# A two-layer decoder trunk on one core: nine chunks of the odd input projection moved between the steps of the differential attention

## The chip, the cores and the metric

The kernel runs on one NeuronCore of one Trainium2 chip, in float32 throughout. The metric is the device time of one execution in microseconds. Large matrix products are made in three matmuls each, from a high and a low part of both operands (high times high, low times high, high times low), so that the single-pass float format reaches nearly float32 accuracy.

## The reference, cut to what matters

Two transformer layers on 512 tokens of width 1024. Each layer has a half-step feed-forward block, a mixer, a cross-attention to a memory of 256 tokens, and another half-step feed-forward block, each between a norm before and a norm after it. The change lies in the mixer of the second (odd) layer:

```python
def odd_mixer(h, w_in, w_out, q_norm, kv_norm, w_uq, w_ukv, lam, subln, rel_tab, lam_init):
    c_q, c_kv, k_rope, qd, kd, vd = split_cols(h @ w_in, OD_SIZES)
    o_c = mla_mixer(c_q, c_kv, k_rope, q_norm, kv_norm, w_uq, w_ukv)
    o_d = diff_mixer(qd, kd, vd, lam, subln, rel_tab[:, A_HEADS + B_HEADS:], lam_init)
    return jnp.concatenate([o_c, o_d], axis=-1) @ w_out

# diff_mixer, per block of 128 queries; q and k have two parts e per head, v one of width 128
s = jnp.einsum('bthed,bshed->behts', qb, k) * scale + rel_bias(dist, tab)
p = masked_softmax(s, dist >= 0)
a = p[:, 0] - lam_full * p[:, 1]
o = jnp.einsum('bhts,bshd->bthd', a, v)
o = rmsnorm(o, subln) * (1.0 - lam_init)
```

`h @ w_in` has 2048 padded output columns, 16 chunks of 128: two for c_q, one for c_kv, one for k_rope, four each for the queries, keys and values of the four differential heads.

## The kernel before, in words

Everything is kept transposed: a chunk is 128 features on the partitions by 512 tokens. The kernel is written by hand for each engine, with semaphores between them; nothing but that written order decides when something runs.

**The weight stream.** A chunk's weights (128 x 1024, 512 KB) are a unit. SP loads units into a ring of four raw buffers (`stream`, L530); GpSimd splits each into `w_hi` (L604) and `w_lo` (L606) in a ring of four (`split`, `units`), as soon as TensorE has finished the unit four before; TensorE makes 8 products of three matmuls from it (`product`, L755 to L757) and signals `unit_done`; VectorE then takes the bank out, times the norm factor r (`leave`, L1742), and signals `chunk_out`.

**The odd mixer** (`odd_mixer` in each engine's block). TensorE makes chunks 0 to 3 in halves inside `pre_norm`, chunk 4 in a spare bank (7), and then all others in turn through banks 0 to 3 (`chunks`). Between them stand the column sums (L783) and transposes (L791) for the norms of c_q and c_kv. VectorE takes the chunks out, makes the norms' inverse roots (`rsqrt`, L1613 to L1631), scales c_q and c_kv (L1975) and forms their low parts `cq_lo` and `ckv_lo` (L1980). When all 16 chunks are made, TensorE transposes the four value chunks (`turn_rows`, L964) in banks 6 and 7, and ScalarE copies them to `diff_v` (`copy_rows`, L1362).

**The differential attention** (`attention(2)`). 32 jobs in this order: head, block of 128 queries i (with 128(i+1) keys), part e. Each is a pipeline over steps; in step s
- TensorE makes the logits of job s (L993), the transposes of job s-4 (L1007) and the value product of job s-6 (L1024); the last two only for e = 1, where both parts have been joined;
- VectorE inverts the row sum of job s-3 (L1844) and scales its probabilities (L1860 for e = 0, L1854 for e = 1, joined with those of e = 0), and adds the bias to the logits of job s and finds their maximum (L1834);
- ScalarE copies the transposed probabilities of job s-4 (L1413) and makes the exponentials of job s (L1400).

Logits go through banks 0, 1, 2 and 5 in turn (`B_S`), outputs through 3 and 4 by head, r through 5. Behind the last step ScalarE takes the last head out (L1422, L1423), TensorE makes the column sums of the subnorm (L1182) and goes on with the query up-projection of MLA (L755 to L757 from `cq_hi`, `cq_lo`), whose results VectorE and GpSimd turn into rotary queries; then comes the MLA attention, with the same pipeline.

Of the kernel before, what the change touches and what calls it, by code (L numbers as in the profile page):

```python
# [27 lines left out]
P = 128  # L28
D, T, MEM, DFF, DEPTH = 1024, 512, 256, 2816, 2
KC = D // P  # L30
NT = T // P
# [3 lines left out]
A_HEADS, B_HEADS, C_HEADS, D_HEADS, X_HEADS = 8, 8, 8, 4, 4  # L35
# [15 lines left out]
R = 4  # L51
# [12 lines left out]
IQ, IK, VG, KB, QB, KCMP, VCMP, KS, VS, KW, VW, QA = 0, 2, 3, 4, 5, 9, 10, 11, 12, 13, 14, 15  # L64

CQ, CKV, KR, DQ, DK, DVT = 0, 2, 3, 4, 8, 12


C_ID, C_CAUSAL, C_ROPE, C_END = 0, P, P + T, P + 3 * T
# [49 lines left out]
def build(nc, a):  # L119
# [151 lines left out]
    def bank_of(name, c, half=0):  # L271

        kind = name.rstrip("0123")
        if kind in ("up", "ev_in", "od_in") and c == R:
            return B_SPARE
        if kind == "down" and c == KC - 1 and half == 1:
            c -= 1
        return (CHUNK[name] + c) % R
# [8 lines left out]
    def post_buf(s, c):  # L287

        return (step[0], step[1], sq[0], sq[1])[c - 4] if len(HALVED[s]) > 1 else sq[1]
    B_S = [(0, 1, 2) if n == 3 else (0, 1, 2, 5) for n in range(5)]  # L290

    sems = {}

# [185 lines left out]
    def out_rows(phase, f):  # L479

        if JOBS[phase][0][0] != "mla":
            return slice(0, P), f
        return slice(DV // 2 * (f % 2), DV // 2 * (f % 2) + DV // 2), f // 2

    def probs_of(phase, s):

# [33 lines left out]
    with nc.Block() as block:  # L520
# [230 lines left out]
        def _(pe):  # L751
# [205 lines left out]
                    half_sums(8, 1)  # L957
                    turn_half(8, 1)

            def turn_rows(key, k, src, tiles):  # L960

                n = TURN[key] + k
                for i in range(tiles):
                    mm = pe.transpose(bank[B_T[n % 2]][:, P * i:P * i + P], src[:, P * i:P * i + P], ident[:])  # L964
                mm.then_inc(turned, 1)

            def attention(phase, hooks={}):
# [4 lines left out]
                def logit(s):  # L972
                    j, info = j0 + s, infos[s]
                    banks = B_S[phase]
                    if s >= len(banks):
                        pe.wait_ge(logit_done, j - len(banks) + 1)
                    if info["mask"] is not None and JOBS[phase][s][1] == 0:
                        pe.wait_ge(mask_done, JOBS[phase][s][2])
                    if phase == 2 and s == 3:
                        pe.wait_ge(lo_done, SPLIT["ckv"] + 1)  # L980
                    out = bank[banks[s % len(banks)]][:, 0:info["w"]]
                    if phase == 0 and JOBS[0][s][2] == 0 and JOBS[0][s][0] in ("slc", "dsa"):
                        pe.wait_ge(q_lo_done, info["strip"] + 1)
                    if phase == 0 and s in (1, 2, 3, 4):
                        pe.wait_ge(k_lo_pool, 2 * s)
                    if phase == 0 and JOBS[0][s] == ("dsa", 0, 0):
                        pe.wait_ge(k_lo_pool, 9)
                    more = info["mask"] is not None
                    if info["k_lo"] is not None:
                        pe.matmul(out, info["q"], info["k"], start=True, stop=False)  # L990
                        mm = pe.matmul(out, info["q"], info["k_lo"], start=False, stop=not more)
                    else:
                        mm = pe.matmul(out, info["q"], info["k"], start=True, stop=not more)  # L993
                    if info["mask"] is not None:
                        mm = pe.matmul(out, ident_bf[:], info["mask"], start=False, stop=True)
                    mm.then_inc(qk_done, 1)

                def turn(s):
                    j, info = j0 + s, infos[s]
                    if not info["turns"]:  # L1000
                        return
                    t, prob = info["turn"], probs_of(phase, s)
                    pe.wait_ge(scaled, j + 1)
                    if t >= infos[0]["turn"] + 2:
                        pe.wait_ge(probT_copied, t - 1)
                    for b in range(info["blocks"]):
                        mm = pe.transpose(bank[B_T[t % 2]][0:info["rows"], P * b:P * b + P],  # L1007
                                          prob[:, P * b:P * b + info["rows"]], ident[:])
                    mm.then_inc(probT_done, 1)
# [146 lines left out]
            def odd_mixer(s):  # L1156
                pre_norm(s, "od_in")
                c0 = CHUNK["od_in"]
                chunks("od_in", 8, R + 1, h_hi, h_lo)
                pe.wait_ge(sq_done, SQ["cq", 0]["sq"] + 2)  # L1160
                sums(sq[0], NT, True, False)
                sums(sq[1], NT, False, True).then_inc(stat_done, 1)
                chunks("od_in", 12, 8, h_hi, h_lo)
                turn_r(("cq", 0), NT)
                pe.wait_ge(sq_done, SQ["ckv", 0]["sq"] + 1)
                sums(sq[0], NT, True, True).then_inc(stat_done, 1)
                chunks("od_in", OD_IN, 12, h_hi, h_lo)
                pe.wait_ge(mla_ready, 2)
                turn_r(("ckv", 0), NT)
                for h in range(D_HEADS):  # L1170
                    if h >= 2:
                        pe.wait_ge(rows_done, V_ROWS["dv"] + h - 1)
                    pe.wait_ge(chunk_out, c0 + DVT + h + 1)
                    turn_rows("dv", h, od[:, DVT + h, :], NT)
                pe.wait_ge(rows_done, V_ROWS["dv"] + D_HEADS)
                attention(2)

                pe.wait_ge(sub_sq, D_HEADS)
                for h in range(D_HEADS):
                    for i in range(NT):  # L1180
# [71 lines left out]
        def _(act):  # L1252
# [102 lines left out]
                        act.activation(gate[p][:], gate[p][:], ACT.Silu).then_inc(silu_done, 1)  # L1355
                halved_squares(s + 1, f"down{f}", y_ffn)

            def copy_rows(key, k, dst, tiles):
                n = TURN[key] + k
                act.wait_ge(turned, n + 1)  # L1360
                src = bank[B_T[n % 2]][:, 0:P * tiles].rearrange("p (i t) -> p i t", i=tiles)
                act.activation(dst, src, ACT.Copy).then_inc(rows_done, 1)  # L1362

            def copy_half(key, k, dst, frm, to):
# [13 lines left out]
                for k in range(len(STRIPS[phase][1])):  # L1378
                    load_strip(phase, k)

            def attention(phase, hooks={}):
                infos, j0 = INFO[phase], JOB0[phase]
                logits, _, probTs = BUFS[phase]
                if phase in STRIPS:
# [41 lines left out]
                        act.activation(h_hi[rows, chunk, :], src[rows, :], ACT.Copy).then_inc(hi_done, 1)  # L1426

                for s in range(len(infos) + OUT_AT + 1):
                    if TURN_AT <= s < len(infos) + TURN_AT:
                        copy(s - TURN_AT)  # L1430
                    if s < len(infos):
                        exp(s)
                    if s > OUT_AT and infos[s - OUT_AT - 1]["ends"]:
                        output_leaves(s - OUT_AT - 1)
                    if s in hooks:
                        hooks[s]()
# [81 lines left out]
            def odd_mixer(s):  # L1518
# [3 lines left out]
                for k in range(2):  # L1522
                    act.wait_ge(chunk_out, c0 + CQ + k + 1)
                    act.activation(sq[k][:], od[:, CQ + k, :], ACT.Square).then_inc(sq_done, 1)
                act.wait_ge(stat_done, SQ["cq", 0]["stat"] + 1)
                act.activation(sq[0][:], od[:, CKV, :], ACT.Square).then_inc(sq_done, 1)
                for k in range(2):
                    act.wait_ge(mla_ready, k + 1)
                    act.activation(cq_hi[:, k, :], od[:, CQ + k, :], ACT.Copy).then_inc(hi_done, 1)
                for h in range(D_HEADS):  # L1530
                    copy_rows("dv", h, dv[:, h, :, :], NT)
                act.wait_ge(mla_ready, 3)
                act.activation(ckv_hi[:], od[:, CKV, :], ACT.Copy).then_inc(hi_done, 1)
                attention(2)
                act.wait_ge(logit_done, JOB0[3])
                act.dma_start(rope_t[:], a["consts"][:, C_ROPE:C_END].rearrange("p (k t) -> p k t", k=2)).then_inc(aux_in, 16)
                act.dma_start(od_causal[:], a["consts"][:, C_CAUSAL:C_CAUSAL + T]).then_inc(aux_in, 16)
# [55 lines left out]
        def _(dve):  # L1593
# [367 lines left out]
            def odd_mixer(s):  # L1961
                def leave_to(c0, c1):
                    for c in range(c0, c1):
                        leave("od_in", c, c + 1, od[:, c, :], r_sb[:])


                leave_to(0, 8)
                dve.wait_ge(chunk_out, CHUNK["od_in"] + 8)
                for key, d, cs, g0, lo in ((("cq", 0), 2 * P, (CQ, CQ + 1), G_Q, (cq_lo[:, 0, :], cq_lo[:, 1, :])),
                                           (("ckv", 0), P, (CKV,), G_KV, (ckv_lo[:],))):  # L1970
                    rsqrt(key, NT, d)
                    leave_to(*((8, 12) if key[0] == "cq" else (12, OD_IN)))
                    dve.wait_ge(r_turned, SQ[key]["rt"] + 1)
                    for k, c in enumerate(cs):
                        dve.scalar_tensor_tensor(od[:, c, :], od[:, c, :], gains[:, g0 + k:g0 + k + 1], bank[B_RT][:],  # L1975
                                                 ALU.mult, ALU.mult).then_inc(mla_ready, 1)
                    for k, c in enumerate(cs):
                        hi = cq_hi[:, k, :] if key[0] == "cq" else ckv_hi[:]
                        dve.wait_ge(hi_done, SPLIT[key[0]] + k + 1)
                        dve.tensor_tensor(lo[k], od[:, c, :], hi.bitcast(F32), ALU.subtract).then_inc(lo_done, 1)  # L1980
                attention(2)
                rsqrt(("sub", 0), NT * D_HEADS, DV)

                dve.wait_ge(aux_in, AUX["od"])
# [170 lines left out]
```

## Time and profile before

| | us |
|---|---|
| median of 3 runs | 2337.35 (2337.11 to 2339.36) |
| the profiled execution | 2340.13 |
| its span | 2338.2 |
| TensorE busy | 2239.3 (96%) |
| VectorE busy | 1233.2 (53%) |
| ScalarE busy | 541.8 (23%) |
| GpSimd busy | 1368.7 (59%) |

PE is TensorE, DVE VectorE, ACT ScalarE, POOL GpSimd, SP the engine that issues weight loads; PEld is TensorE's loading of stationary operands. Busy times of TensorE are modelled: its matmuls overlap, so the distance between starts is the better measure of what one takes. A float32 matmul of the attention appears as two records, and so does one of the column sums. PEclk is the granted clock of TensorE as a share of 2.4 GHz; it has two levels, 1.00 and 0.50. All positions are us from the span's start. The odd mixer's projection begins near 1567 us and its differential attention ends near 1712 us.

### The profile page before, as it was taken

The numbers are of one execution on the slowest core, as the hardware profiler recorded it, in microseconds if no ns is written. First come the engines' busy times: TensorE is split into PE (matmuls) and PEld (weight loads), VectorE is DVE, ScalarE is ACT, GpSimd is POOL, SyncE is SP. The second block draws the span as 40 slices with busy tenths as digits, with TensorE's granted clock in tenths as the row PEclk, the third lists the DMA queues.
The fourth block names the chain that finished last, engine by engine and source line by source line (L and its number), as shares of the span: only waits on it lengthen the run. The fifth ranks groups of instructions, "written<-read, shape, count | busy, mean of one in ns | idle before, by whom it ended". The sixth has DMA issues, their size and how long they took to land.

```text
span 2338.2 us, 32876 instructions
## 1 busy us (share of the span) xinstructions
PE 2239.3 (96%) x11598; PEld 1893.0 (81%) x11598; DVE 1233.2 (53%) x2370; ACT 541.8 (23%) x1313; POOL 1368.7 (59%) x850
## 2 busy tenths in 40 slices
PE   6999999999999899999999999999989989999997
PEld 5888888778878788888898888888667879888886
DVE  5554324798865575543247454243577645645323
ACT  2101003228742441110030000021346144101000
POOL 5666665671347376666667666666231745766662
PEclk9999999999999999999999999999889999999998
DMA  5433332310123123333323333333111311333331
GB/s 192 170 94 95 92 98 81 131 46 20 46 85 105 55 73 99 99 96 93 98 67 112 95 98 92 99 88 104 50 50 36 109 55 54 109 98 92 93 98 52
DMA packets 62146, 205.61 MB, mean 88 GB/s; under 512 B 6815, under 2 KB 9247, under 8 KB 61652
## 3 DMA queue, kind: packets, MB, share of 16 engines
q1 hardware_dynamic: 55312, 187.86, 26.9%
q10 hardware_dynamic: 6724, 16.29, 2.0%
q8 instruction: 68, 1.11, 0.2%
q14 instruction: 42, 0.34, 0.0%
HBM read 201.98 MB, written 8.70 MB: 90 GB/s over the span
## 4 chain that ended last, share of the span: by engine, by line
PE 85%; DVE 10%; issue 2%; ACT 2%; POOL 1%; DMA 0%; SPq 0%; DVEq 0%; ACTq 0%; POOLq 0%
PE bank L755 25%; PE bank L757 25%; PE bank L756 25%; PE bank L1024 3%; PE bank L1007 2%; PE bank L993 1%; POOL sq_sum L630 1%; DVE ev_logit L1834 1%; DVE h_lo L1647 1%; DVE top L1931 1%; PE bank L783 1%; DVE bank L1708 1%; PE bank L807 1%; DVE od_logit L1834 0%; DVE x_res L1716 0%
## 5 line engine op out<-in xcount | busy, mean ns | idle before, releaser
L606 POOL TENSOR_TENSOR w_lo<-w_raw,w_hi 128x1024 fp32r<-128x1024 f32 (+1 forms) x358 | 866.5, 2420 | 29.9
L755 PE MATMUL bank<-h_hi,w_hi 128*128 128x512 f32 (+1 forms) x2136 | 804.5, 377 | 27.8 <-DVE h_lo L1647 11.5
L756 PE MATMUL bank<-h_lo,w_hi 128*128 128x512 f32 (+1 forms) x2136 | 797.4, 373 | 0.0
L757 PE MATMUL bank<-h_hi,w_lo 128*128 128x512 f32 (+1 forms) x2136 | 797.3, 373 | 0.0
L604 POOL TENSOR_SCALAR w_hi<-w_raw 128x1024 fp32r<-128x1024 f32 (+1 forms) x358 | 383.6, 1071 | 687.2 <-PE bank L757 522.3
L755 PEld LDWEIGHTS bank<-h_hi,w_hi 128*128 128x128 f32 x2136 | 408.4, 191 | 106.5 <-issue 16.4
L757 PEld LDWEIGHTS bank<-h_hi,w_lo 128*128 128x128 f32 x2136 | 408.2, 191 | 69.5
L756 PEld LDWEIGHTS bank<-h_lo,w_hi 128*128 128x128 f32 x2136 | 409.1, 192 | 67.8
L755 PE MATMUL bank<-act_hi,w_hi 128*128 128x512 f32 (+1 forms) x792 | 290.1, 366 | 0.0
L756 PE MATMUL bank<-act_lo,w_hi 128*128 128x512 f32 (+1 forms) x792 | 289.4, 365 | 0.0
L757 PE MATMUL bank<-act_hi,w_lo 128*128 128x512 f32 (+1 forms) x792 | 289.4, 365 | 0.0
L1783 DVE TENSOR_TENSOR up<-bank,r_tok 128x512 f32<-128x512 f32 x88 | 60.6, 689 | 346.7 <-PE bank L757 346.7
L1355 ACT ACTIVATE gate<-gate 128x512 f32<-128x512 f32 x88 | 55.6, 632 | 758.3 <-DVE gate L1781 758.2
L1788 DVE TENSOR_SCALAR act_hi<-up 128x512 f32 (+1 forms) x88 | 192.8, 2191 | 11.8 <-DVE up L1786 11.2
L1759 DVE COPY y_ffn<-bank 128x512 f32<-128x512 f32 x28 | 19.4, 691 | 310.6 <-PE bank L757 310.6
L756 PEld LDWEIGHTS bank<-act_lo,w_hi 128*128 128x128 f32 x792 | 149.4, 189 | 24.3
L755 PEld LDWEIGHTS bank<-act_hi,w_hi 128*128 128x128 f32 x792 | 149.3, 189 | 24.2
L757 PEld LDWEIGHTS bank<-act_hi,w_lo 128*128 128x128 f32 x792 | 149.3, 189 | 23.8
L1750 DVE TENSOR_TENSOR sq_sum<-sq_sum,sq 128x512 f32<-128x512 f32 x42 | 103.0, 2452 | 27.9 <-ACT sq L1333 27.9
L1786 DVE TENSOR_TENSOR up<-gate,up 128x512 f32<-128x512 f32 x88 | 103.4, 1175 | 6.5 <-ACT gate L1355 1.3
L1333 ACT ACTIVATE sq<-y_ffn 128x512 f32<-128x512 f32 x24 | 15.2, 633 | 343.8 <-DVE y_ffn L1759 343.8
L1790 DVE TENSOR_TENSOR act_lo<-up,act_hi 128x512 f32 (+1 forms) x88 | 76.1, 865 | 9.4
(275 smaller groups left out, 2421.6 us busy)
## 6 DMA issues: line engine op xcount, KB each, us to landing
w_raw<-in_w_up SPq DMA_DIRECT2D x176, 512.0 KB, 3.6
w_raw<-in_w_down SPq DMA_DIRECT2D x64, 448.0 KB, 3.3
w_raw<-in_w_down SPq DMA_DIRECT2D x32, 512.0 KB, 3.5
w_raw<-in_w_ev_in SPq DMA_DIRECT2D x19, 512.0 KB, 3.6
w_raw<-in_w_xkv SPq DMA_DIRECT2D x16, 512.0 KB, 3.5
w_raw<-in_w_od_in SPq DMA_DIRECT2D x16, 512.0 KB, 3.5
bias_line_rows<-bias_lines ACTq DMA_DIRECT2D x1, 6400.0 KB
ev_strip<-bias_line_rows ACTq DMA_DIRECT2D x16, 256.0 KB, 2.9
```

The source lines that it names most:

```text
L604: pool.tensor_scalar(w_hi[j][:, 0:cols], raw[j][:, 0:cols], 1.0, 0.0, ALU.mult, ALU.add).then_inc(hi_split, 1)
L606: pool.tensor_tensor(w_lo[j][:, 0:cols], raw[j][:, 0:cols], w_hi[j][:, 0:cols].bitcast(F32), ALU.subtract).then_inc(split_done, 1)
L755: pe.matmul(out, w_hi[j][:, w], hi, start=first, stop=False)
L756: pe.matmul(out, w_hi[j][:, w], lo, start=False, stop=False)
L757: return pe.matmul(out, w_lo[j][:, w], hi, start=False, stop=last)
L1024: mm = pe.matmul(bank[B_O[chunk % 2]][features, tokens], v, probTs[t % N_PROBT][0:info["rows"], P * b:P * b + P], start=info["opens"] and ...
L1355: act.activation(gate[p][:], gate[p][:], ACT.Silu).then_inc(silu_done, 1)
L1750: dve.tensor_tensor(sq_sum[:], sq_sum[:], sq[c % 2][:], ALU.add).then_inc(sq_added, 1)
L1783: dve.tensor_tensor(up[p][:], bank[(c0 + k + 1) % R][:], r_sb[:], ALU.mult).then_inc(chunk_out, 1)
L1786: dve.tensor_tensor(up[p][:], gate[p][:], up[p][:], ALU.mult).then_inc(prod_done, 1)
L1788: dve.tensor_scalar(act_hi[:, 2 * i + n, :], up[p][:], 1.0, None, ALU.mult).then_inc(act_hi_done, 1)
L1790: dve.tensor_tensor(act_lo[:, 2 * i + n, :], up[p][:], act_hi[:, 2 * i + n, :].bitcast(F32), ALU.subtract).then_inc(act_done, 1)
```

## The change

Only chunks 0 to 6 are made before the attention; the other nine (7 to 15) are made inside it, one to three products at the end of each of its 32 steps (`OD_FILL`: 3 in each of the first eight, 3 and 2 in turn in the next sixteen, 1 in each of the last eight). The order of the weights' chunks is changed on the host, so that the first seven are c_q, c_kv and then query, key and value of head 0 and the query of head 1; then key and value of head 1 and so on, and k_rope last. The nine chunks alternate between banks 0 and 1, and the logits of this attention have banks 2 and 5 only. VectorE takes each of the nine out at the end of the step after the one in which it ends. The value chunks of heads 1 to 3 are transposed at the end of steps 6, 16 and 24, in the transposes' bank that is not in use, and copied by ScalarE at the start of the same steps in its own order. The sums for the norm of c_q come before chunk 5, those for c_kv before chunk 6.

```diff
+OD_ORDER = (CQ, CQ + 1, CKV) + tuple(t + h for h in range(D_HEADS) for t in (DQ, DK, DVT)) + (KR,)
+OD_FIRST = 7
+OD_FILL = (3,) * 8 + (3, 2) * 8 + (1,) * 8
@@ bank_of
+        if kind == "od_in" and c >= OD_FIRST:
+            return (c + 1) % 2
-    B_S = [(0, 1, 2) if n == 3 else (0, 1, 2, 5) for n in range(5)]
+    B_S = [(0, 1, 2, 5), (0, 1, 2, 5), (2, 5), (0, 1, 2), (0, 1, 2, 5)]
@@
+    fill_of, fill_end, n_fill = [], {}, 8 * OD_FIRST
+    for at_step, count in enumerate(OD_FILL):
+        fill_of.append([divmod(n, KC) for n in range(n_fill, n_fill + count)])
+        n_fill += count
+        for c, k in fill_of[-1]:
+            if k == KC - 1:
+                fill_end[c] = at_step
+    DV_STEP = {h: 2 * (fill_end[OD_ORDER.index(DVT + h)] // 2) + 2 for h in range(1, D_HEADS)}
+    def dv_bank(h):
+        return B_T[(INFO[2][DV_STEP[h] - TURN_AT - 1]["turn"] + 1) % 2 if h else TURN["dv"] % 2]
@@ TensorE, attention
-                    if phase == 2 and s == 3:
-                        pe.wait_ge(lo_done, SPLIT["ckv"] + 1)
+                    if phase == 2 and s == 1:
+                        pe.wait_ge(mla_ready, 3)
+                    if phase == 2 and JOBS[2][s][2] == 0 and JOBS[2][s][0] == "diff0":
+                        pe.wait_ge(chunk_out, CHUNK["od_in"] + OD_ORDER.index(DK + JOBS[2][s][1]) + 1)
...
+                    if phase == 2 and s + TURN_AT - 1 in DV_STEP.values():
+                        pe.wait_ge(rows_done, V_ROWS["dv"] + 1 + list(DV_STEP.values()).index(s + TURN_AT - 1) + 1)
@@ TensorE, odd_mixer
-                chunks("od_in", 8, R + 1, h_hi, h_lo)
                 pe.wait_ge(sq_done, SQ["cq", 0]["sq"] + 2)
                 sums(sq[0], NT, True, False)
                 sums(sq[1], NT, False, True).then_inc(stat_done, 1)
-                chunks("od_in", 12, 8, h_hi, h_lo)
+                u0 = UNIT["od_in"]
+                chunk_of_unit(u0 + 5, c0 + 5, (u0 + 5) % R, bank_of("od_in", 5), h_hi, h_lo)
                 turn_r(("cq", 0), NT)
                 pe.wait_ge(sq_done, SQ["ckv", 0]["sq"] + 1)
                 sums(sq[0], NT, True, True).then_inc(stat_done, 1)
-                chunks("od_in", OD_IN, 12, h_hi, h_lo)
+                pe.wait_ge(chunk_out, c0 + OD_ORDER.index(DVT) + 1)
+                turn_rows("dv", 0, od[:, DVT, :], NT)
+                chunk_of_unit(u0 + 6, c0 + 6, (u0 + 6) % R, bank_of("od_in", 6), h_hi, h_lo)
                 pe.wait_ge(mla_ready, 2)
                 turn_r(("ckv", 0), NT)
-                for h in range(D_HEADS):
-                    if h >= 2:
-                        pe.wait_ge(rows_done, V_ROWS["dv"] + h - 1)
-                    pe.wait_ge(chunk_out, c0 + DVT + h + 1)
-                    turn_rows("dv", h, od[:, DVT + h, :], NT)
-                pe.wait_ge(rows_done, V_ROWS["dv"] + D_HEADS)
-                attention(2)
+                pe.wait_ge(rows_done, V_ROWS["dv"] + 1)
+                def fill(step_):
+                    for h, at_ in DV_STEP.items():
+                        if at_ == step_:
+                            pe.wait_ge(chunk_out, c0 + OD_ORDER.index(DVT + h) + 1)
+                            turn_rows("dv", h, od[:, DVT + h, :], NT, dv_bank(h))
+                    for c, k in fill_of[step_] if step_ < len(fill_of) else ():
+                        if k == 0:
+                            pe.wait_ge(split_done, u0 + c + 1)
+                            pe.wait_ge(chunk_out, c0 + c - 1)
+                        mm = product(bank_of("od_in", c), (u0 + c) % R, k, h_hi[:, k, :], h_lo[:, k, :],
+                                     k == 0, k == KC - 1)
+                        if k == KC - 1:
+                            mm.then_inc(unit_done, 1)
+                attention(2, {n: lambda n=n: fill(n) for n in range(len(JOBS[2]))})
+                pe.wait_ge(chunk_out, c0 + OD_IN)
@@ ScalarE, odd_mixer
-                for h in range(D_HEADS):
-                    copy_rows("dv", h, dv[:, h, :, :], NT)
+                copy_rows("dv", 0, dv[:, 0, :, :], NT)
...
-                attention(2)
+                attention(2, early={at_: lambda h=h: copy_rows("dv", h, dv[:, h, :, :], NT, dv_bank(h))
+                                    for h, at_ in DV_STEP.items()})
@@ VectorE, odd_mixer
-                leave_to(0, 8)
-                dve.wait_ge(chunk_out, CHUNK["od_in"] + 8)
+                leave_to(0, 5)
+                dve.wait_ge(chunk_out, CHUNK["od_in"] + 5)
...
-                    leave_to(*((8, 12) if key[0] == "cq" else (12, OD_IN)))
+                    leave_to(*((5, 6) if key[0] == "cq" else (6, 7)))
...
-                attention(2)
+                attention(2, {at_ + 1: lambda c=c: leave_to(c, c + 1) for c, at_ in fill_end.items()})
+                dve.wait_ge(chunk_out, CHUNK["od_in"] + OD_IN)
@@ host
-    ins["w_od_in"] = tiles(np.concatenate(cols, 1), KC, OD_IN)
+    ins["w_od_in"] = tiles(np.concatenate(cols, 1), KC, OD_IN)[list(OD_ORDER)]
```

## Rows read from the trace of the kernel before

**Rows 1.** The page's chain that ended last, by engine.
```profile
PE 85%; DVE 10%; issue 2%; ACT 2%; POOL 1%; DMA 0%; SPq 0%; DVEq 0%; ACTq 0%; POOLq 0%
```

**Rows 2.** Windows: length; busy PE, PEld, DVE, ACT, POOL; PEclk; DMA share, GB/s.
```profile
1663.50:1712.30 48.80, 39.04 (x201) 26.48 (x198) 35.50 (x147) 32.04 (x93) 0.00 (x0) 0.79 0.04 13
1667.50:1709.20 41.70, 33.04 (x161) 21.62 (x161) 34.01 (x145) 28.19 (x86) 0.00 (x0) 0.78 0.03 7
1713.40:1724.60 11.20, 11.18 (x44) 10.08 (x45) 4.43 (x14) 0.00 (x0) 0.00 (x0) 0.55 0.20 69
431.00:457.00 26.00, 24.97 (x132) 17.00 (x125) 23.73 (x29) 10.71 (x24) 12.60 (x8) 1.00 0.28 82
1750.00:1780.00 30.00, 29.44 (x203) 23.81 (x202) 26.58 (x96) 23.97 (x70) 0.00 (x0) 1.00 0.05 18
```

**Rows 3.** Timeline of TensorE around the attention: start, us, what, [idle before].
```profile
1663.35 1.04 PE L964 MATMUL bank<-ident,od_proj 128*128 128x128 f32 x8
...
1666.47 0.92 PE L993 MATMUL bank<-od_proj 64*128 64x128 f32 x6 [0.69 <-ACT diff_v L1362]
...
1707.26 0.63 PE L1007 MATMUL bank<-ident,od_prob 128*128 128x128 f32 x3 [2.02 <-DVE od_prob L1854]
```

**Rows 4.** Timeline of VectorE in the projection: chunks 5 and 6 leave.
```profile
1605.51 0.69 DVE L1742 TENSOR_TENSOR od_proj<-bank,r_tok 128x512 f32<-128x512 f32 x1 [4.75 <-PE bank L757]
1610.95 0.69 DVE L1742 TENSOR_TENSOR od_proj<-bank,r_tok 128x512 f32<-128x512 f32 x1 [4.75 <-PE bank L757]
```

**Rows 5.** Chain in order of time, attention stages: start, us, what.
```profile
1687.84 1.16 PE bank L993 x4
...
1692.11 0.89 PE bank L1024 x8
1693.00 1.11 PE bank L993 x4
...
1762.45 0.44 PE bank L1007 x4
```

**Rows 6.** The same chain in the projection: sums, r transposes, next matmul.
```profile
1616.35 1.68 PE bank L783 x16
...
1639.95 0.44 PE bank L791 x4
1640.39 0.79 PE bank L783 x8
1641.18 0.34 PE bank L755
```

**Rows 7.** VectorE's cq_lo (ns min/median/max), and GpSimd's timeline beside it.
```profile
L1980 DVE TENSOR_TENSOR cq_lo<-od_proj,cq_hi x2: 678/1439/2200, 1642.0 to 1644.2; 128x512 fp32r<-128x512 f32 x2
...
1640.15 1.05 POOL L604 TENSOR_SCALAR w_hi<-w_raw 128x1024 fp32r<-128x1024 f32 x1 [1.91 <-PE bank L757]
1641.29 2.40 POOL L606 TENSOR_TENSOR w_lo<-w_raw,w_hi 128x1024 fp32r<-128x1024 f32 x1
```

**Rows 8.** Timeline of TensorE in the even mixer: twelve matmuls between small ones.
```profile
431.18 0.50 PE L755 MATMUL bank<-h_hi,w_hi 128*128 128x512 f32 x1
...
434.13 0.71 PE L1085 MATMUL bank<-ev_proj 32*128 32x256 f32 x8
```

**Rows 9.** Chain in order of time, from the second last logit to the sums.
```profile
1704.46 0.67 DVE od_logit L1834
...
1712.28 0.35 ACT diff_o L1422
...
1713.42 6.11 PE bank L1182 x32
```

**Rows 10.** The same chain behind the sums: two matmuls of the query projection.
```profile
1720.60 0.43 PE bank L757
...
1725.06 0.24 PE bank L756
```

**Rows 11.** VectorE's logit group, 1667.5 to 1709.2: busy, mean ns, idle before.
```profile
L1834 DVE CUSTOM_DVE_ANT_0 od_logit<-bank,od_strip 128x128 f32<-128x128 f32 (+3 forms) x32 | 15.4, 486 | 5.4 <-PE bank L993 5.4
```

More of the change, by code:

```diff
@@ L483, in out_rows @@
         return slice(DV // 2 * (f % 2), DV // 2 * (f % 2) + DV // 2), f // 2
+    fill_of, fill_end, n_fill = [], {}, 8 * OD_FIRST
[5 more added lines that the diff above has]
+                fill_end[c] = at_step
+    assert n_fill == KC * OD_IN
+    DV_STEP = {h: 2 * (fill_end[OD_ORDER.index(DVT + h)] // 2) + 2 for h in range(1, D_HEADS)}
+    def dv_bank(h):
+        return B_T[(INFO[2][DV_STEP[h] - TURN_AT - 1]["turn"] + 1) % 2 if h else TURN["dv"] % 2]
     def probs_of(phase, s):
@@ L958, in ffn, with turn_rows @@
                     turn_half(8, 1)
-            def turn_rows(key, k, src, tiles):
+            def turn_rows(key, k, src, tiles, to=None):
                 n = TURN[key] + k
+                to = B_T[n % 2] if to is None else to
                 for i in range(tiles):
-                    mm = pe.transpose(bank[B_T[n % 2]][:, P * i:P * i + P], src[:, P * i:P * i + P], ident[:])
+                    mm = pe.transpose(bank[to][:, P * i:P * i + P], src[:, P * i:P * i + P], ident[:])
                 mm.then_inc(turned, 1)
@@ L1356, in ffn, with copy_rows @@
                 halved_squares(s + 1, f"down{f}", y_ffn)
-            def copy_rows(key, k, dst, tiles):
+            def copy_rows(key, k, dst, tiles, frm=None):
                 n = TURN[key] + k
                 act.wait_ge(turned, n + 1)
-                src = bank[B_T[n % 2]][:, 0:P * tiles].rearrange("p (i t) -> p i t", i=tiles)
+                src = bank[B_T[n % 2] if frm is None else frm][:, 0:P * tiles].rearrange("p (i t) -> p i t", i=tiles)
                 act.activation(dst, src, ACT.Copy).then_inc(rows_done, 1)
@@ L1379, in first_strips, with attention @@
                     load_strip(phase, k)
-            def attention(phase, hooks={}):
+            def attention(phase, hooks={}, early={}):
                 infos, j0 = INFO[phase], JOB0[phase]
@@ L1428, in attention @@
                 for s in range(len(infos) + OUT_AT + 1):
+                    if s in early:
+                        early[s]()
                     if TURN_AT <= s < len(infos) + TURN_AT:
@@ L1524, in odd_mixer @@
                     act.activation(sq[k][:], od[:, CQ + k, :], ACT.Square).then_inc(sq_done, 1)
+                act.wait_ge(chunk_out, c0 + CKV + 1)
                 act.wait_ge(stat_done, SQ["cq", 0]["stat"] + 1)
@@ L1963, in leave_to @@
                     for c in range(c0, c1):
-                        leave("od_in", c, c + 1, od[:, c, :], r_sb[:])
-                leave_to(0, 8)
-                dve.wait_ge(chunk_out, CHUNK["od_in"] + 8)
+                        leave("od_in", c, c + 1, od[:, OD_ORDER[c], :], r_sb[:])
+                leave_to(0, 5)
+                dve.wait_ge(chunk_out, CHUNK["od_in"] + 5)
                 for key, d, cs, g0, lo in ((("cq", 0), 2 * P, (CQ, CQ + 1), G_Q, (cq_lo[:, 0, :], cq_lo[:, 1, :])),
```

## Prediction

> **What bounds the kernel now.** I read the page's chain of waits first: 85% of the span is TensorE, 10% VectorE [rows 1]. So a change is worth what it takes out of TensorE's sequence at the place where it acts. Next the windows by stage. In the differential attention with what leads into it (1663.5 to 1712.3 us) TensorE is busy 39.0 of 48.8 us at a mean granted clock of 0.79, and GpSimd does nothing [rows 2]. The timeline shows why: TensorE waits for VectorE's scaled probabilities (2.02 us before 1707.26) and, at the start, for ScalarE's copies of the values (0.69) [rows 3]. The projection before it has no such holes: its chunks leave at a steady 5.44 us [rows 4]. The change puts projection work into the hole. What can be won is the hole (idle time, and time lost to the half clock), less what the interleaving costs.
>
> **Work per piece.** A chunk is 24 matmuls and takes 5.44 us (its results leave at 1605.51 and 1610.95) [rows 4]; nine are 48.96 us, before and after. A product (three matmuls) is 0.68 us. The attention's own TensorE work at the full clock, by head [rows 5]: logits have four records of each width; 512 columns take 1.11, 256 columns 1.16 at the half clock, so 0.58, 384 between them 0.84, and 128 columns I put at the 0.11 a record of the value product: 3.0 us. Ten transposes at 0.11 (four in 0.44) are 1.1, twenty records of the value product at 0.11 (eight in 0.89) 2.2. That is 6.3 us a head, 25.2 us for four, where 45.8 us pass now from the first logit (1666.47 [rows 3]) to the last value product (ended 1712.28 [rows 9]).
>
> **Up to the new first logit.** The spare chunk, number 4, ends 5.44 before the exit at 1605.51, at 1600.07 [rows 4]. Then, in the new order: eight column sums 1.68; chunk 5, 5.44 + 0.11 (the first matmul behind small ones takes 0.34, not 0.23), to 1607.3; transposes of r 0.44, the ckv sums 0.79, to 1608.5 [rows 6]; chunk 5, now the first value chunk, has left by 1608.0, so its four transposes go at once, 0.5 (eight in 1.04 [rows 3]), to 1609.0; chunk 6 with its first matmul to 1614.55; transposes of r 0.44: the attention starts at 1615.0. VectorE beside it scales cq (two operations), makes two cq_lo (2.9 us [rows 7]) and ten small rsqrt operations, from 1608.1 to about 1614.3, just in time for r. The sums and r transposes that stood between later chunks are the same instructions, moved and not added.
>
> **The interleaved stretch.** From 1615.0 TensorE has 48.96 (chunks) + 25.2 (attention) + 1.5 (three value chunks transposed, 0.5 each), and a price for each of the 32 visits to the chunks. The trace has one such interleaving, in the even mixer: twelve matmuls from 431.18 to the next small one at 434.13, 2.95 us where 12 x 0.227 = 2.72 [rows 8], so 0.23 a visit. The least is nothing, if weight loads hide it, or a little under it if fills hide weight loads of the attention; I keep 0 to 0.23 as ends and take 0.23, since that row has just this pattern: 31 x 0.23 = 7.1 up to the last logit. Behind the last logit are left one product, 9 transposes and 20 value records, 0.7 + 1.0 + 2.2 = 3.9. The last logit is done at 1615.0 + 48.96 + 25.2 + 1.5 + 7.1 - 3.9 = 1693.9.
>
> **The waits that it adds.** A chunk's first product waits for the split weights and for the chunk two before it to have left its bank. Behind that wait are all later logits and transposes on TensorE, and VectorE and ScalarE behind them. GpSimd needs 1.05 + 2.40 = 3.4 us a unit [rows 7] and now has about 9 us for one; VectorE's exit follows the chunk, and TensorE comes back to the bank a whole chunk later: nothing. SP's loads come later with the splits, nothing else stands behind them. With two logit banks a logit waits for VectorE's read of the one two steps before; steps are 2.3 to 2.9 us (1.7 in the last eight), VectorE's mean step now is 41.7/32 = 1.3 [rows 2]: nothing, unless VectorE becomes slow (third rival). ScalarE's value copies, waited for at steps 7, 17 and 25, have a fill of 0.7 to 2 us in front of the wait. Against all of it I put 0.5 us; the bounds are 0 and 2.8, four waits (r and three copies) as long as the 0.69 before the first logit now [rows 3].
>
> **The drain.** Behind the last logit no fill helps. VectorE has a logit 0.7 [rows 9], a scale of the step before 1.0, the exit of chunk 15 0.7, scales 0.7 and 1.15; then transposes 0.55, ScalarE's copy 0.6, value product 1.1: 6.5 us. Now it is 1704.46 to 1712.28, 7.8 us, with a backlogged VectorE and the clock partly at half [rows 9]. End at 1693.9 + 6.5 + 0.5 = 1700.9 against 1712.28: **11.4 us gained**.
>
> **Behind it.** The subnorm's 16 sums take 6.11 us, 0.38 each [rows 9], against 0.21 each in the row of eight [rows 6]: the granted clock is 0.55 from 1713.4 to 1724.6 [rows 2], mostly the lower level (1.2 GHz). The first twelve matmuls of the query projection come 0.43 apart and not 0.23 [rows 10]. At 2.4 GHz it would be 2.7 + 2.4 = 5.1 us less. Before the fall TensorE did only the drain and a wait of 1.2 us. The new kernel has the same drain, wait and sums, so the nearest row says no gain; as the stretch before them is dense now, I take 1.0 of the 0 to 5.1. All later work hangs on these sums (rsqrt, rope, GpSimd's additions) and moves with them, and the chain stays TensorE's: the gain passes whole. Sum: 11.4 + 1.0 = 12.4 us. The profiled execution took 2340.13 us (span 2338.2), 2327.7 by it; against the median of the runs, 2337.35, it is **2325.0 us**.
>
> **Rivals.**
> 1. *The clock stays up through the drain and the sums.* For: the fills keep TensorE dense until step 31. Against: drain and sums are the same sparse work as now. It gives 11.4 + 5.1 = 16.5: 2320.9 us. Chance 0.14.
> 2. *The clock falls inside the stretch, and the kernel gets slower.* Transposes and short matmuls stand between the fills, and the fills thin out. Whatever full-clock work runs at 1.2 GHz costs its own length again. Steps 16 to 31 hold 28 products (19.0 us), two heads less the drain (8.7) and 16 visits (3.7), 31.4 us: 31.4 - 12.4 = 19.0 slower, 2356 us. It decides from 12.4 us of such work on. Against: the even mixer's interleaving (431 to 457) ran at 1.00, and the MLA stage (1750 to 1780), all short matmuls and transposes, at 1.00 too [rows 2]. Chance 0.05. The Trainium skill speaks for this rival: "TensorE: Matmul & The Clock Gate", Part 4: PE-mode transpose, says that a transpose does not count as activity for the clock; the MLA stage's trace shows that transposes among matmuls need not pull it down.
> 3. *VectorE becomes the bound.* GpSimd is idle in this stretch now and will split some twelve units in it, 12 x 3.4 = 41 us. Two cq_lo operations are alike, but one took 678 and the other 2200 ns, beside GpSimd's w_lo at 1641.29 [rows 7]. VectorE takes 41.7 us for the attention's steps [rows 2], 5.4 of it waiting for logits [rows 11]; 36 and nine exits (6.2) make 42. If it stood still whenever GpSimd works, 42 + 41 = 83 us from about 1617.5 put the last logit at 1700.5, 6.1 later than above with its 0.5: gain 6.3, 2331.1 us. Against: one of the two cq_lo and most of VectorE's operations beside GpSimd kept their time. Chance 0.13. The Trainium skill, "SBUF — State Buffer", Who interferes with whom, says that only operations with two SBUF inputs or in a two-port mode are shut out; by that the logits, which read PSUM (15.4 us), would go on undisturbed and this rival stays small.
>
> **How the numbers follow.** Forecast 0.68, own range 2321.5 to 2328.5 (visits from 0 to 7.1, waits to 2.8, clock 0 to 5.1, not all at one end). A measurement of this kernel can tell about 0.2%, 4.7 us, from no change. Faster: forecast, rival 1 and most of rival 3, 0.91; within: the rest of rival 3, 0.04; slower: rival 2, 0.05. Range for 8 in 10: 2319.5 (rival 1 and cheaper visits) to 2331 (nearly all of rival 3).
>
> **What would show it.** First new logit near 1615; TensorE without holes over 0.3 us to 1694 at clock 1.00; VectorE waiting for TensorE there, not the reverse; 0.2 us a visit; last value product near 1701; the sums near 6 us. Wrong would be: TensorE idle before transposes inside the stretch (rival 3), a granted clock under 1 before the drain (rival 2), or a first logit after 1618 (r or the value copies late).

## The result

The changed kernel takes 2339.65 us (median of 20 runs, 2338.05 to 2341.9) against 2336.87 us (20 runs, 2331.96 to 2339.38): ratio 1.0015, 95% interval 1.0009 to 1.0021. It is slower, by 0.15%; forecast were 2325.0 us and a range that ended at 2331. The runs of the kernel before fall into two groups, near 2332 us at a mean granted clock of 0.986 and near 2337 us at 0.980 to 0.985 (as its runs beside the experiments show), while those of the changed one stay together at 0.984 to 0.987. The profiled execution took 2339.66 us with a span of 2337.7.

The chain by engine is the same as in [rows 1]. The windows of the changed kernel, in the columns of [rows 2]: from the first logit to the end of the last one, the drain behind it, and from the subnorm's sums to the end of the query projection.

```profile
1614.70:1706.70 92.00, 89.51 (x382) 57.78 (x382) 48.99 (x145) 30.70 (x86) 30.88 (x18) 1.00 0.19 55
1706.70:1714.41 7.71, 6.00 (x32) 5.03 (x32) 3.69 (x11) 2.64 (x7) 0.00 (x0) 0.78 0.00 0
1715.64:1728.20 12.56, 12.56 (x57) 11.04 (x58) 5.77 (x17) 0.00 (x0) 1.84 (x2) 0.73 0.17 61
```

The change did what it says: the hole is gone, TensorE is busy 89.5 of 92.0 us at the full clock, and the first logit came at 1614.7 (forecast 1615.0). But the stretch lasts 92.0 us where 78.9 were forecast. The last value product ends at 1714.41, which is 2.1 us behind that of the kernel before (1712.28 [rows 9]), and not 11.4 ahead. So nearly all the time is in TensorE's own work, and the chain in order of time shows in which part (start, us, what; step 13 and the logit of step 14, then the end):

```profile
1655.78 0.84 PE bank L1015 x2
1656.62 0.26 PE bank L1031
1656.88 0.89 PE bank L1048 x8
1657.77 0.24 PE bank L774
...
1659.17 1.05 PE bank L1015 x2
1660.22 0.43 PE bank L774
...
1711.38 3.01 PE bank L1048 x14
...
1715.64 4.91 PE bank L1220 x32
```

L1015 is the logit (L993 before), L1031 the transpose, L1048 the value product, L774 to L776 the chunks' matmuls, L1220 the subnorm's sums. In [rows 5] four records of 512 columns, the logits of both parts, take 1.11 us together. Here the two records of **one** part take 1.05. All 32 logits of this chain say the same: 0.42, 0.63, 0.84 and 1.05 us for one part of 128, 256, 384 and 512 columns (within 0.02), 23.5 us in all. The first matmul behind a logit takes 0.43 and not 0.23; behind a value product it takes 0.24. The first transpose behind a logit takes 0.26 where one takes 0.11 in [rows 5].

The two parts of a head lie in rows 0 to 63 and 64 to 127 of `od`, and their contraction has 64 rows. In the old order the logit of part 1 followed that of part 0 directly, since even steps have nothing but their logit. The change put a fill between them.

### The profile page after: what moved, and what is told of

The parts are those of the page before. It is cut to its first block, busy times and chain, and to the rows that moved or that the text cites. A ratio compares the mean times of both kernels' runs of the same rounds, so it can differ in the third digit from the quotient of the medians.

```text
span 2337.7 us, 32872 instructions
## 1 busy us (share of the span) xinstructions
PE 2241.2 (96%) x11594; PEld 1882.6 (81%) x11598; DVE 1246.2 (53%) x2370; ACT 543.7 (23%) x1313; POOL 1368.8 (59%) x850
## 3 DMA queue, kind: packets, MB, share of 16 engines
q8 instruction: 68, 1.11, 0.2%
## 4 chain that ended last, share of the span: by engine, by line
PE 85%; DVE 10%; issue 2%; ACT 2%; POOL 1%; DMA 0%; another core or an unknown queue 0%; SPq 0%; DVEq 0%; ACTq 0%; POOLq 0%
PE bank L774 25%; PE bank L775 25%; PE bank L776 25%; PE bank L1048 3%; PE bank L1015 2%; PE bank L1031 2%; DVE h_lo L1688 1%; DVE ev_logit L1875 1%; POOL sq_sum L649 1%; DVE top L1972 1%; PE bank L802 1%; DVE bank L1749 1%; DVE x_res L1757 1%; PE bank L826 0%; ACT h_hi L1305 0%
## 5 line engine op out<-in xcount | busy, mean ns | idle before, releaser
L774 PE MATMUL bank<-h_hi,w_hi 128*128 128x512 f32 (+1 forms) x2136 | 806.2, 377 | 27.9 <-DVE h_lo L1688 11.2
L776 PE MATMUL bank<-h_hi,w_lo 128*128 128x512 f32 (+1 forms) x2136 | 796.0, 373 | 0.0
L774 PEld LDWEIGHTS bank<-h_hi,w_hi 128*128 128x128 f32 x2136 | 407.1, 191 | 112.7 <-issue 22.1
L776 PEld LDWEIGHTS bank<-h_hi,w_lo 128*128 128x128 f32 x2136 | 406.8, 190 | 69.5
L774 PE MATMUL bank<-act_hi,w_hi 128*128 128x512 f32 (+1 forms) x792 | 290.1, 366 | 0.0
L776 PE MATMUL bank<-act_hi,w_lo 128*128 128x512 f32 (+1 forms) x792 | 289.4, 365 | 0.0
L774 PEld LDWEIGHTS bank<-act_hi,w_hi 128*128 128x128 f32 x792 | 149.3, 189 | 24.3
L776 PEld LDWEIGHTS bank<-act_hi,w_lo 128*128 128x128 f32 x792 | 149.3, 189 | 23.9
L1831 DVE TENSOR_TENSOR act_lo<-up,act_hi 128x512 f32 (+1 forms) x88 | 76.2, 866 | 9.4
```

The source lines that it names most:

```text
L774: pe.matmul(out, w_hi[j][:, w], hi, start=first, stop=False)
L776: return pe.matmul(out, w_lo[j][:, w], hi, start=False, stop=last)
L1831: dve.tensor_tensor(act_lo[:, 2 * i + n, :], up[p][:], act_hi[:, 2 * i + n, :].bitcast(F32), ALU.subtract).then_inc(act_done, 1)
```

## The experiments

Theory A: neighbouring logits on different halves of the rows run side by side; the fill between them ended that. Theory B: the number of visits to the chunks costs, whatever stands beside them. Theory C: the added waits cost. All kernels are variants of the changed one if nothing else is said.

| kernel | median us (runs) | ratio to before, 95% | first to last logit start, us |
|---|---|---|---|
| changed | 2339.65 (20) | 1.0009 to 1.0021 | 91.4 |
| fills behind odd steps (16 visits) | 2332.26 (12) | 0.9977 to 1.0 | 86.7 |
| pairs kept, 32 visits | 2329.67 (12) | 0.9963 to 0.9984 | 81.5 |
| values later | 2335.67 (12) | 0.9996 to 1.0017 | 88.8 |
| 16 visits, same rows | 2339.59 (11) | 1.001 to 1.003 | 89.8 |
| pairs kept, values later | 2325.93 (5), again 2324.8 (5) | 0.9951 to 0.9977, 0.9941 to 0.9968 | 76.2 |
| the same, tail filled | 2325.45 (5) | 0.9951 to 0.9976 | 75.2 |
| 16 visits, values later | 2327.28 (7) | 0.9958 to 0.998 | 77.5 |
| before, same rows | 2341.66 (10) | 1.0027 to 1.0063 | 54.8, mostly at the lower clock (37.3 before) |
| changed, same rows | 2338.64 (11) | 1.001 to 1.0028 | 91.3 |

The last column is taken from the logit records of each profile. The ratio is to runs of the kernel before beside each set of experiments; its medians were 2336.38 us beside the first four, 2332.93 beside the next four and 2335.43 beside the last two (the control and the repeat). Where the profiled execution is far from the median, its own time is given.

**Fills behind odd steps only.**
```diff
-OD_FILL = (3,) * 8 + (3, 2) * 8 + (1,) * 8
+OD_FILL = (0, 6) * 4 + (0, 5) * 8 + (0, 2) * 4
```


> The changed kernel, but every fill stands behind the odd steps only (6, 5 and 2 products where it was 3+3, 3+2 and 1+1), so that the logits of the two parts of a head and block follow each other on TensorE as in the kernel before, and there are 16 visits to the chunks instead of 32. Theory A (the two parts' logits read different halves of the rows, and side by side they cost less than apart: four records of 512 columns took 1.11 us together before, and two of them take 1.05 now): the four records are back near 1.1 us, plus one entry, and the last logit ends 10 to 12 us earlier than 1706.7; the whole is 8 to 12 us faster than the changed kernel, 2328 to 2332. Theory B (only the number of visits costs, about 0.4 us for each of the 16 that go; the adjacency does nothing by itself): 6 us earlier, 2333 to 2335, and four records of 512 columns take 1.7 us or more. Theory C (what delays the stretch is VectorE and the waits for the value chunks): under 2 us.

Measured 2332.26, 7.4 us under the changed kernel, a little less than A's 8 to 12. The chain of this kernel, then that of the one with the same rows below it (a pair of logits of 128 columns, then the three of the last head with 256, 384 and 512, in each):

```profile
1642.85 0.42 PE bank L1015 x4
...
1694.30 0.63 PE bank L1015 x4
...
1697.59 0.84 PE bank L1015 x4
...
1700.98 1.11 PE bank L1015 x4
```
```profile
1641.17 0.64 PE bank L1015 x4
...
1694.36 1.06 PE bank L1015 x4
...
1698.07 1.48 PE bank L1015 x4
...
1702.10 1.91 PE bank L1015 x4
```

A pair of 512 costs 1.11 again, hardly more than one part alone in the changed kernel; B said 1.7. But in the profiled execution the stretch got only 4.7 us shorter and not 10 to 12. There TensorE waited 4.4 us for VectorE's exits ahead of the value transposes (2.5 in the changed kernel), and behind the first two of these waits the clock fell, for 6.8 us and for 3.4. At half the clock 10.2 us hold the work of 5.1, so about 5 us went this way (an estimate from the two levels). That execution took 2337.69 us, 5.4 more than the median, so the typical run lost less. The first of the two falls:

```profile
1633.28 1.00 PE L984 MATMUL bank<-ident,od_proj 128*128 128x128 f32 x4 [1.40 <-DVE od_proj L1783]
1634.21 2.07 PE L1015 MATMUL bank<-od_proj 64*128 64x512 f32 x2
```
```profile
1633.20:1640.20 7.00, 6.92 (x18) 4.42 (x19) 2.07 (x8) 2.38 (x6) 0.00 (x0) 0.52 0.26 75
```

**Pairs kept, 32 visits.** The fill of an even step moves behind the logit of the next odd one.
```diff
                     if s < n:
                         logit(s)
+                    if s in mids:          # step s + 1: fill(s) for even s
+                        mids[s]()
                     if TURN_AT <= s < n + TURN_AT:
                         turn(s - TURN_AT)
```


> The changed kernel with its 32 visits of the same size, but the fill of each even step stands behind the logits of the next odd step, so only the adjacency of the two parts' logits is restored. Theory A (adjacent logits on different row halves run side by side): 5.4 us from the pairs and about 3 from the logits that no longer stand between two fills, 7 to 9 us earlier; 2331 to 2334. Theory B (visits alone cost): 0 to 2 us, 2338 to 2341. If A holds and the visits cost too, this one is 3 us behind the kernel with 16 visits.

Measured 2329.67, and a stretch 9.9 us shorter than the changed kernel's, with the same fills and visits. That is more than A's 7 to 9, and B's 0 to 2 is excluded. By the chain the logits take 14.1 us where they took 23.5. The edit does a little more than restore the pairs: a fill now stands between the logits and the transposes behind them, and three of these take 0.33 and four 0.44 where it was 0.48 and 0.59 (13 times 0.15, 2.0 us). Against it, the clock fell here too, for 3.4 us behind the wait at step 6 (the profiled execution took 2331.51 us).

**Values later.**
```diff
-    DV_STEP = {h: 2 * (fill_end[OD_ORDER.index(DVT + h)] // 2) + 2 for h in range(1, D_HEADS)}
+    DV_STEP = {h: 2 * (fill_end[OD_ORDER.index(DVT + h)] // 2) + 4 for h in range(1, D_HEADS)}
```


> The changed kernel, with the value chunks of heads 1 to 3 transposed two steps later (8, 18 and 26 instead of 6, 16 and 24). In the changed kernel TensorE stands 1.4 and 1.1 us before the transposes of steps 6 and 24, because VectorE takes the chunk out only after that same step's logit. Theory A and B alike: both waits vanish, the last logit comes 2 to 2.5 us earlier, 2337 to 2338. Theory C (the waits are what ate the gain): 8 us or more earlier.

The waits of 2.5 us ahead of L984 vanished and the stretch became 2.6 us shorter; 2335.67 is 4 us under the changed kernel, whose runs are of another set; by the two ratios to the kernel before (1.0006 and 1.0015) it is about 2. So the waits that C names are real and cost these 2.6 us, but they are not what ate the gain: C had said 8 or more.

**16 visits, same rows.**
```diff
-            s.update(q=od[64 * e:64 * e + DH, DQ + h, q], k=od[64 * e:64 * e + DH, DK + h, 0:w], ...
+            s.update(q=od[0:DH, DQ + h, q], k=od[0:DH, DK + h, 0:w], ...
```


> The kernel with fills behind odd steps only (16 visits, adjacent logits), but both parts of a head take the query and key of the first part, rows 0 to 63, so that the second part's logits are computed from the wrong rows; everything else is the same work. Theory A (rows): adjacency no longer helps, a pair of 512 columns takes 1.7 us or more instead of 1.1, and the kernel is 4.5 to 6 us slower than the one with 16 visits and the right rows. Theory B (adjacency helps by fewer visits or by keeping one kind of matmul together, whatever the rows): same time as that one within 1 us.

It takes 2339.59, 7.3 us more than the same kernel with the right rows (forecast 4.5 to 6), and the second fence above is its chain: the pairs stand together and cost 1.91 us where 1.11 was. By widths the difference is 0.80 + 0.64 + 0.43 + 0.22 = 2.1 us a head, 8.4 for four; three of the pairs are split by value transposes in both kernels, which leaves 7.1 here. So most of what made the pairs cheap is the rows. But not all: the four pairs of a head take 5.1 us together on the same rows and 5.9 apart, so 0.8 us a head, 3.2 for four, come from the neighbourhood alone, one change into a logit (0.2) in place of two.

**Pairs kept, values later.** The pairs kernel with both; the value chunks are also transposed ahead of their step's logit, so that they break no pair.
```diff
                 for s in range(n + OUT_AT):
+                    if s in pre:           # DV_STEP: turn_rows("dv", ...)
+                        pre[s]()
                     if s < n:
                         logit(s)
```


> The kernel with pairs kept and 32 visits, with the value chunks of heads 1 to 3 transposed two steps later and ahead of that step's logit, so that they neither wait for VectorE nor stand between a pair. If the terms add up (waits 2.5 us, three broken pairs 1 to 1.5, the 1.2 us GpSimd or clock effects around them): the last logit ends 3 to 4 us earlier than 82.2 us after the first one, the whole is 2326 to 2328. If VectorE is what paces the stretch now (the rival), nothing changes.

Measured 2325.93. The last logit ends at 1691.43 (its row of the chain, then stretch and drain as windows cut at 1691.90), 76.8 us after the first one begins, and the drain takes 7.6. The stretch is 2.1 us less than the prediction gave it and 5.4 less than the 82.2 above, where 3 to 4 were forecast. Of these 5.4, some 1.7 are the fall of the clock in the kernel with pairs, which this one does not have.

```profile
1690.32 1.11 PE bank L1015 x4
```
```profile
1614.60:1691.90 77.30, 76.31 (x381) 55.13 (x381) 51.93 (x142) 29.10 (x82) 30.74 (x18) 1.00 0.22 65
1691.90:1699.00 7.10, 4.99 (x34) 3.86 (x32) 4.31 (x15) 3.76 (x9) 0.00 (x0) 1.00 0.00 0
```

**The same, tail filled.**
```diff
-OD_FILL = (3,) * 8 + (3, 2) * 8 + (1,) * 8
+OD_FILL = (3,) * 8 + (3, 2) * 8 + (0, 1) * 4 + (1, 1, 1, 0, 1)
...
-                attention(2, {at_ + 1: ... for c, at_ in fill_end.items()})
+                attention(2, {at_ + 1: ... for c, at_ in fill_end.items() if c < OD_IN - 1})
+                leave_to(OD_IN - 1, OD_IN)
```


> As the previous one, and the last chunk (the rotary key) is spread over the end: one product in each second step of the last head and four in the drain, where TensorE waits for VectorE; VectorE takes it out behind the last scale, during the subnorm's sums, and TensorE waits for that exit only before the query projection. If the drain is bound by VectorE and ScalarE as read (7.7 us for 3.9 us of TensorE work), the four products leave the path (2.7 us) and so does the exit (0.6 us): 3 us faster than the previous one, and up to 5 more where the clock then stays up through the sums. If the last steps are bound by VectorE already, only the exit's 0.6 us is won.

2325.45, the same within the spread; the 3 us did not come. With fewer fills in the last head TensorE waited for VectorE there (1.1 us before a logit, 0.4 before the transposes behind it, 0.9 in the drain), and two products stood in front of the last transposes. The clock is the more telling part: the drain ran at full clock, and at the sums behind it the clock fell to the lower level all the same. The windows are the drain, then the sums with the start of the query projection:

```profile
1691.00:1698.40 7.40, 6.49 (x41) 5.28 (x39) 4.46 (x15) 3.75 (x9) 0.00 (x0) 1.00 0.00 0
1699.50:1711.00 11.50, 11.45 (x45) 10.20 (x46) 4.62 (x15) 0.00 (x0) 0.00 (x0) 0.56 0.19 68
```

**16 visits, values later.** The kernel with pairs kept and values later, with the `OD_FILL` of the first experiment.

> The kernel with fills behind odd steps only (16 visits), with the value chunks transposed two steps later and ahead of the logit. The first such kernel stood 4.4 us waiting for VectorE's exits and 10 us of it ran at the half clock, from the wait at step 6 on. If those were the whole reason why it lost to the kernel with 32 visits: now 16 visits beat 32 by 16 x 0.2 = 3 us, 2324 to 2326. If large fills themselves starve VectorE and then TensorE (three to four microseconds without a logit), it stays behind the one with 32 visits.

2327.28: the waits of 4.4 us and the low clock in the stretch are gone, but 16 visits do not beat 32. TensorE waits 3.6 us for probabilities (2.1 with 32). Before the transposes at 1658.24 it waits 1.04 us for a scale of 384 columns that took VectorE 2.83 us (from 1655.35) beside GpSimd's w_lo (from 1655.39, 2.38 us); alone such a scale takes 0.62. And half the visits saved next to nothing: what costs is the change into a logit (0.2) and out of one, 0.2 to a chunk's matmul, 0.15 to a transpose (0.26 for the one above behind a logit, 0.11 [rows 5] else). In the pairs kernel each pair has one change in and one out, however many visits there are.

**The kernel before, same rows.** The same edit in the kernel before the change; both parts take the first part's query and key.

> The kernel before the change, with the query and key of the first part taken for both parts, rows 0 to 63, so that the second part's logits are computed from the wrong rows; no chunk is moved. Theory A (pairs on different row halves run side by side): a pair of 512 columns takes 1.7 us or more instead of 1.11 at the full clock, 5.4 us more TensorE work in the stage, of which its idle 8 us may hide some: 1 to 5 us slower, 2338 to 2341. Theory B: the records' times and the whole are unchanged.

2341.66 (2337.84 to 2359.47). Four records of 512 columns at the full clock, against 1.11 in [rows 5] (1.13 in the view used here, where a record runs on into the next):

```profile
1671.14 1.98 PE L993 MATMUL bank<-od_proj 64*128 64x512 f32 x4
```

So the kernel before has the gain of the pairs too. The median is 8.7 us over that of the kernel before beside it, where 1 to 5 were forecast. Part of it may be the clock: at like mean clocks (0.982 to 0.984) the difference of the medians is about 4.6 us (2341.42 against 2336.81). So how much of the 8.4 us of added work the hole took up is not shown. The profiled execution took 2357.59 us and ran at the lower clock nearly throughout the attention, though TensorE hardly paused:

```profile
1681.00:1729.00 48.00, 47.33 (x135) 30.20 (x134) 24.36 (x95) 20.30 (x58) 0.00 (x0) 0.50 0.00 1
```

**The changed kernel, same rows (control), and the best one again.**

> A control: the changed kernel itself, with the query and key of the first part taken for both parts, rows 0 to 63, so that the second part's logits are computed from the wrong rows. Theory A (only neighbouring logits on different row halves run side by side, and the changed kernel has none): nothing is left to lose, two records of 512 columns still take 1.05 us, and the time stays within 1 us of the changed kernel's, 2338 to 2341. If the rows cost something else than the pairing (reading the same rows again, the clock), it is slower here too, by the 7 us that separated the two kernels with pairs.

> The kernel with pairs kept, 32 visits and the value chunks two steps later once more, beside the control on one chip: 2324 to 2327 us, 12 to 15 us under the control.

2338.64 and 2324.8. With no pairs left there was nothing to lose: two records of 512 columns take 1.05 us as in the changed kernel (from the control's chain), and the ratio to before, 1.001 to 1.0028, overlaps the changed kernel's. Between this and the best kernel lie 13.8 us.

```profile
1658.42 1.05 PE bank L1015 x2
```

## Why the prediction was wrong

**The step that failed** is the term "logits ... 3.0 us" a head in "Work per piece". It was read from four-record rows and carried into an order in which these records no longer stand together. Apart they are 2 x (0.42 + 0.63 + 0.84 + 1.05) = 5.9 us a head, 11.5 us more in all: 8.4 of it because the two parts no longer run side by side on their two halves of the rows, 3.2 because each part now pays for its own change into a logit (both by the kernel with 16 visits and the same rows; the sum is rounded). The rows gave a sign that was not followed up: in [rows 5] four logit records of 512 columns take 1.11 us, and four value records of 128 columns, a quarter as wide, would take 0.44; at that price four of 512 would be 1.8.

The account of the 13.1 us that the stretch (92.0 against 78.9) took more, from the chain of the changed kernel:

| term, up to the end of the last logit | forecast | measured | more |
|---|---|---|---|
| logits, with the change into each | 12.0 | 23.5 | 11.5 |
| chunks, with the price of the visits | 55.4 (48.3 + 7.1) | 52.2 (3.0 of it behind 15 logits) | -3.2 |
| transposes and value products of the attention | 10.0 | 12.0 (2.0 of it behind 13 logits) | 2.0 |
| value chunks transposed | 1.5 | 1.9 | 0.4 |
| waits ahead of the value transposes | 0 (0.5 were put behind the stretch) | 2.5 | 2.5 |

The last column adds to 13.2, as the rows of the chain are rounded. The runs confirm the account: with the pairs together (and a fill behind each, which frees the transposes) the stretch was 9.9 us shorter, and with the values later as well another 5.3, in which the waits, the last three split pairs and the clock's fall are together.

Point by point:
- *What bounds the kernel, the hole, the start at 1615.0*: right, to 0.3 us.
- *A chunk 5.44 us, no wait for splits or banks, steps not paced by VectorE*: right. TensorE waits for VectorE only where chunks are still to leave.
- *0.23 us a visit*: wrong as a price of every visit. It hangs on the neighbour: none behind a value product, 0.2 behind a logit, 3.0 us in all and not 7.1. What was over here hid part of what was missing at the logits, where each change into one costs 0.2 (in the first row of the table).
- *The value copies have a fill in front of them*: right; but the wait that came is another: the value chunk's exit stands in VectorE's order behind the logit of the very step at whose end TensorE wants to transpose it. Its upper bound of 2.8 us held (2.5).
- *Drain 6.5 us*: right at the full clock. In the kernel with the values later it took 6.5 (1703.51 to 1709.97, clock 1.00); here it took 7.7, since the clock fell in it to a mean of 0.78 (3.01 us for the last 14 value records, 1.84 there). With pairs it takes 7.6 at the full clock, as both logits of the last pair stand at its head.
- *Sums and query projection 1.0 us faster*: 1.6 (13.8 us from the last value product to 1728.2; 15.4 before). The clock was at 1.00 for the first 1.4 us of the sums and at 0.50 in their last 2; they took 4.91 us.
- *Rival 1, the clock stays up*: no. Even behind a drain full of matmuls the sums fell to the lower level.
- *Rival 2, the clock falls inside the stretch*: not in the changed kernel (1.00 throughout). It did behind a wait in the first 16-visit kernel and, for 3.4 us, in the first kernel with pairs; that shows a fall and not that thin fills cause it. What makes it fall in one execution and not in another stays open.
- *Rival 3, VectorE is the bound*: no. It was busy 49.0 of 92.0 us, and none of its joined scales took over 0.75. In kernels with pairs some of them took 2.6 to 2.8 beside w_lo, and with 16 visits one of these held TensorE up for 1.04 us, so the mechanism exists; it is a small part.
- *The 12.4 us that could be won*: they were counted against one execution of 2340.13 us at a mean clock of 0.980, while the 20 runs of the kernel before have a median of 2336.87 and seven of them lie near 2332. So part of what the forecast would win may not be lost in every run; no profile was taken of a run near 2332, so where those save is not shown.

The right rival, that the change takes from the logits their neighbour, was not among the three. The order of the changed kernel was in the diff, and the shapes "64*128" in the rows. The Trainium skill, "TensorE: Matmul & The Clock Gate", Part 3: Packing small matmuls — row/col tiling, says that matmuls on different row groups of the array run at the same time. The traces agree: two parts on the two halves take 1.11 us together, both on the same half 1.91, and apart 1.05 each.

## What to carry to other kernels

Before something is put between two instructions of an engine, ask what these two gain from each other, and compare what a neighbour costs alone and in its group; a group's row gives the price of the group only. A change of order that leaves such groups whole, with the value chunks later, gained 0.36% and 0.45% in its two comparisons, where 0.53% were forecast; the same amount of moved work that split them lost it all. Place a consumer two steps behind its producer's exit, and not one, where the exit waits in another engine's order.

## What the runs showed of the hardware

- Two float32 matmuls of 64 rows, 512 columns: 1.06 to 1.11 us together on different halves of the rows, 1.91 on the same half, 1.05 for one alone between other matmuls.
- A float32 matmul of 64 rows beside chunk matmuls costs 0.2 us at each side (the first chunk matmul behind it takes 0.43 and not 0.23), and 0.15 ahead of a transpose; value products, float32 too but with 128 rows, cost nothing there.
- VectorE's joined scale of 384 columns, with both inputs in SBUF, took 0.62 us, and 2.83 beside GpSimd's w_lo.
- TensorE stayed at the lower clock for 48 us while busy 47.3 of them, in the kernel before with both parts on rows 0 to 63 (2357.59 us; its median run took 2341.66). Why it fell into this is open.
- During the one-column sums, 32 records back to back with TensorE never idle, the clock fell to the lower level, or was there already, in every kernel profiled: they took 4.8 to 6.6 us, where 0.21 for each of the 16 would be 3.4.
